# The second feed-forward product as seven block products in place of eight, in a two-layer hybrid decoder trunk

## The chip, the cores and the metric

The kernel is one program on one core of a Trainium2 chip. The time is that of the device for one launch, in microseconds; of the kernel before there are three runs, and their median counts.

## The reference

Each of two layers takes a stream x of 512 tokens x 1024 channels, float32. Three token mixers (gated spatial MLP, latent attention with eight heads, gated DeltaNet) read one normed input projection; their outputs are gated, merged, multiplied by W_out and added to x. Then comes the part that the change touches:

```
h2 = rms_norm(x, norm2_g[l])
x = x + jnp.square(jax.nn.relu(h2 @ w_ff1[l])) @ w_ff2[l]
```

w_ff1 is 1024 x 4096, w_ff2 4096 x 1024. The output is x after the second layer.

## The kernel before

**Precision.** Every large product is made in three passes over operands split into a high part (fp32r) and a low part (what the rounding left): high by high, high by low, low by high. `passes` (L454) issues the three. ScalarE or VectorE split the activations; GpSimd splits the weights, one unit of 128 x 1024 at a time: `high` (L424) copies the raw weights to wHi, `low` (L429) subtracts wHi from the raw ones into wLo. Raw units arrive by DMA in two slots, split ones stand in a ring of four. A unit is split when the unit four places earlier is done on TensorE.

**Layout.** The stream is channel-major: xT is 8 tiles of 128 channels x 512 tokens. The weights are stationary, the tokens move, 512 columns a matmul.

**The feed-forward block.** For each quarter of the 4096 hidden channels, TensorE makes eight hidden tiles (`ff1`, one unit and 24 matmuls each) and then eight units of the second product (`wide_sums`, L485, 24 matmuls each), which sums eight hidden tiles into eight banks of output channels. For a hidden tile, VectorE rectifies and scales it out of PSUM into relu (L2018), squares it back into PSUM (L2020) and subtracts the high part (L2023); ScalarE squares it into the high part (L1458). After a quarter VectorE adds eight banks to xT (L2034).

**Order.** Each engine has its own program, written out by hand, and executes it strictly in order; semaphores with absolute counts join them. No scheduler is used. The next norm's work hangs on the second product's end: `stream_low` on VectorE (adds the bank to xT, L1518, low part of h, L1504, accumulates squares, L1511) and `stream_high` on ScalarE (high part of h, copy to xT, square; L1115, L1116, L1109). The factor of the norm is applied after the product, so the next layer's first unit ("misc") begins before the statistic (`sum_stream`, L482) is known. At the very end `last_sums` interleaves the transposes back to token-major (`turn_out`, L542, L533), which ScalarE copies to ost and DMAs store.

## Time and profile before

| | us |
|---|---|
| median of three runs (1796.21 to 1796.32) | 1796.24 |
| profiled execution: span, first to last instruction | 1793.5 |
| profiled execution's own time: the page gives its span alone; median less span | 2.7 |
| TensorE busy | 1776.8 |
| GpSimd busy | 1030.1 |
| VectorE busy | 856.7 |
| ScalarE busy | 466.6 |
| granted TensorE clock, mean | 1.000 |

The busy shares add up every record of an engine, without counting an overlap twice. Matmuls overlap in the records: one is listed with its whole way through the array, though the next starts earlier. So a mean duration of a matmul isn't what it costs; the distance between starts is. The chain of waits is followed back from the last instruction. An idle time of an engine that isn't in the chain costs nothing.

### The profile page before, as it was taken

How to read it: one execution, taken by the hardware profiler on the slowest of the kernel's cores; microseconds unless marked ns; L12 is line 12 of the kernel's file. 1: busy time of each engine (PE TensorE's matmuls, PEld its weight loads, DVE VectorE, ACT ScalarE, POOL GpSimd, SP SyncE). 2: the span in 40 equal slices, each digit the busy share in tenths (PEclk: the TensorE clock that was granted, in tenths of full speed). 3: DMA queues.
4: the chain of work that ended last, by engine and by line, in shares of the span. 5: the costliest groups of instructions: out<-in, count | busy, mean ns of one | idle time of the engine just before them, and what ended most of it. 6: DMA issues, size and time to landing. Idle time of an engine off the chain costs nothing.

```text
span 1793.5 us, 26458 instructions
## 1 busy us (share of the span) xinstructions
PE 1776.8 (99%) x10078; PEld 1449.8 (81%) x10078; DVE 856.7 (48%) x1436; ACT 466.6 (26%) x922; POOL 1030.1 (57%) x580
## 2 busy tenths in 40 slices
PE   8999999999999999999999999999999999999999
PEld 7777888788888888888877788887888888888887
DVE  8786626644444231314276964466435351414141
ACT  6423317641113000000155142266311130001011
POOL 6543466255666666666664435652556666666663
PEclk9999999999999999999999999999999999999999
DMA  6222132132333333333342212320323333333332
GB/s 233 94 71 72 58 96 94 36 118 83 94 94 109 101 99 94 94 101 99 94 141 71 83 49 73 104 83 26 128 89 100 94 94 94 97 103 94 94 96 80
DMA packets 48439, 167.25 MB, mean 93 GB/s; under 512 B 5136, under 2 KB 10544, under 8 KB 47824
## 3 DMA queue, kind: packets, MB, share of 16 engines
q1 hardware_dynamic: 47024, 156.42, 28.1%
q10 hardware_dynamic: 1312, 9.33, 1.4%
q8 instruction: 80, 1.31, 0.3%
q14 instruction: 23, 0.19, 0.0%
HBM read 159.44 MB, written 6.29 MB: 92 GB/s over the span
## 4 chain that ended last, share of the span: by engine, by line
PE 94%; DVE 3%; ACT 2%; issue 1%; DMA 0%; SPq 0%; DVEq 0%; ACTq 0%
PE ps L461 28%; PE ps L463 27%; PE ps L462 27%; PE ps L967 2%; PE ps L976 1%; PE ps L989 1%; DVE acc L1511 1%; DVE hLo L1504 1%; PE ps L740 1%; PE ps L727 0%; PE ps L777 0%; DMA xin<-x 0%; PE ps L1039 0%; PE ps L763 0%; PE ps L752 0%
## 5 line engine op out<-in xcount | busy, mean ns | idle before, releaser
L429 POOL TENSOR_TENSOR wLo<-wraw,wHi 128x1024 fp32r<-128x1024 f32 x288 | 721.9, 2507 | 23.9
L424 POOL TENSOR_SCALAR wHi<-wraw 128x1024 fp32r<-128x1024 f32 x288 | 308.2, 1070 | 714.1 <-PE ps L463 698.4
L461 PE MATMUL ps<-hHi,wHi 128*128 128x512 f32 x1360 | 554.0, 407 | 1.3 <-DVE convd L1633 1.3
L463 PE MATMUL ps<-hHi,wLo 128*128 128x512 f32 x1360 | 530.4, 390 | 0.0
L462 PE MATMUL ps<-hLo,wHi 128*128 128x512 f32 x1360 | 529.8, 390 | 0.0
L461 PEld LDWEIGHTS ps<-hHi,wHi 128*128 128x128 f32 x1360 | 255.4, 188 | 61.7 <-issue 7.7
L462 PEld LDWEIGHTS ps<-hLo,wHi 128*128 128x128 f32 x1360 | 255.7, 188 | 55.4 <-issue 4.6
L463 PEld LDWEIGHTS ps<-hHi,wLo 128*128 128x128 f32 x1360 | 255.2, 188 | 54.5
L461 PE MATMUL ps<-fHi,wHi 128*128 128x512 f32 x640 | 249.3, 390 | 0.0
L463 PE MATMUL ps<-fHi,wLo 128*128 128x512 f32 x640 | 249.0, 389 | 0.0
L462 PE MATMUL ps<-fLo,wHi 128*128 128x512 f32 x640 | 249.0, 389 | 0.0
L1458 ACT ACTIVATE fHi<-relu 128x512 fp32r<-128x512 f32 x64 | 40.6, 635 | 555.3 <-DVE relu L2018 555.3
L2034 DVE TENSOR_TENSOR xT<-xT,ps 128x512 f32<-128x512 f32 (+1 forms) x57 | 38.6, 678 | 256.6 <-PE ps L463 256.6
L463 PEld LDWEIGHTS ps<-fHi,wLo 128*128 128x128 f32 x640 | 120.1, 188 | 25.1
L462 PEld LDWEIGHTS ps<-fLo,wHi 128*128 128x128 f32 x640 | 120.1, 188 | 24.8
L461 PEld LDWEIGHTS ps<-fHi,wHi 128*128 128x128 f32 x640 | 120.1, 188 | 24.8
L2018 DVE SCALAR_TENSOR_TENSOR relu<-ps,rstdT 128x512 f32<-128x512 f32 x64 | 44.3, 692 | 193.8 <-PE ps L463 185.9
L1166 ACT ACTIVATE sg<-ps 128x512 f32<-128x512 f32 x48 | 28.8, 600 | 255.7 <-DVE ps L1576 255.7
L1576 DVE TENSOR_TENSOR ps<-ps,rstdT 128x512 f32<-128x512 f32 x56 | 39.0, 699 | 111.2 <-PE ps L463 111.0
L463 PE MATMUL ps<-bHi,wLo 128*128 128x512 f32 x192 | 74.7, 389 | 0.0
L461 PE MATMUL ps<-bHi,wHi 128*128 128x512 f32 x192 | 74.7, 389 | 0.0
L462 PE MATMUL ps<-bLo,wHi 128*128 128x512 f32 x192 | 74.7, 389 | 0.0
(312 smaller groups left out, 1928.9 us busy)
## 6 DMA issues: line engine op xcount, KB each, us to landing
wraw<-stream SPq DMA_DIRECT2D x288, 512.0 KB, 3.5
out<-xT ACTq DMA_DIRECT2D x2, 2048.0 KB, 8.8
xT<-out ACTq DMA_DIRECT2D x2, 2048.0 KB, 8.6
xin<-x SPq DMA_DIRECT2D x4, 512.0 KB, 6.6
out<-ost SPq DMA_DIRECT2D x2, 512.0 KB, 3.0
out<-ost SPq DMA_DIRECT2D x3, 256.0 KB, 2.2
prm<-params ACTq DMA_DIRECT2D x1, 647.0 KB, 4.0
prm<-params SPq DMA_DIRECT2D x1, 576.0 KB, 8.9
```

Of the source, the lines that this page charges most:

```text
L424: nc.gpsimd.tensor_scalar(wHi[:, slot], wraw[:, slot % RAW], 1.0, 0.0, ALU.mult, ALU.add).then_inc(unit_high, 1)
L429: nc.gpsimd.tensor_tensor(wLo[:, slot], wraw[:, slot % RAW], wHi[:, slot].bitcast(F32), ALU.subtract).then_inc(unit_split, 1)
L461: mm(o, lh[lc], rh[rc], start=start, stop=False)
L462: mm(o, lh[lc], rl[rc], start=False, stop=False)
L463: return mm(o, ll[lc], rh[rc], start=False, stop=stop)
L740: last = mm(half_bank(half, 1)[hs(m), j % 2 * 64:j % 2 * 64 + 64], gated[hs(m), m // 2, 0, h], r[hs(m), j] if m else rhsv[hs(m), 0, h * 64 ...
L967: mm(bank[:, 0:w], qhT[0:QK, h, i * P:w], khT[0:QK, h, 0:w], start=True, stop=True).then_inc(score_done, 1)
L1166: f(gate[:, d % 2], bank_of(TILE_NO[tile]), ACT.Sigmoid).then_inc(bank_read[TILE_NO[tile] % 2], 1)
L1458: f(fHi[q % 2][:, n], relu[:, n % 2], ACT.Square).then_inc(f_hi, 1)
L1576: return tt_(o, bank_of(TILE_NO[tile]), rstdT[:], ALU.mult)
L2018: stt(relu[:, n % 2], bank_of(n), 0.0, rstdT[:], ALU.max, ALU.mult).then_inc(relu_done, 1)
L2034: tt_(xT[:, d][part], xT[:, d][part], sums_bank(d)[part], ALU.add).then_inc(x_added, 1)
```

## The change

The second product runs in 8 groups, each over four hidden tiles (512 hidden channels), on blocks of 256 tokens x 256 hidden channels by 256 hidden x 512 output channels. By hand that would be eight block products; Strassen's scheme in Winograd's form needs seven, of sums and differences of blocks. In the names: p1 to p7 are the seven products of a group, f0 to f3 the four hidden tiles of the next group that stand between them. A product is 2 token tiles x 2 hidden tiles x 3 passes = 12 matmuls of 512 columns. Now the activations are stationary and the weights move, and the result is token-major, in `y` (4 tiles of 128 tokens x 1024 channels).

- The hidden tiles are mixed on VectorE (`mix_halves`) and split into seven kinds of stationary blocks (fHi, fLo): kinds 0 and 1 from the first two tiles of a group, 2 to 6 from the last two (4 to 6 are the mixed ones).
- The weight blocks are loaded as four tiles (w11, w12, w21, w22). Their sums: B on GpSimd (`sum_upper`), T3 and T2 (`sum_lower`) and T4 (`sum_corners`) on VectorE.
- The high part of every weight unit from here on is copied by ScalarE (`high_part`), its low part made by GpSimd (`low_part`).
- The products of a chain share PSUM banks: X takes p1, p6, p7 and p4, one after another, and VectorE adds the bank to y after each (`add_corner`), 256 tokens at a time, in the last group 128.
- The stream is turned to token-major at the start of each feed-forward block (`turn_residual`: 32 transposes, four copies by ScalarE) and turned back between the layers (`turn_stream`). After the last layer y is stored as it is; `last_sums`, `turn_out` and the copies to ost are gone.
- Some semaphores are joined into others outside the block (vector_step); no instruction moves by that.

```diff
+PLACES = ("p1", "f0", "p5", "p6", "f1", "p2", "p7", "f2", "p3", "p4", "f3")
+LAST_PLACES = ("p2", "p1", "p6", "p7", "p4", "p5", "p3")
...
+            def low_part(layer, group, place, source):
+                at = split_no(group, place)
+                pool.wait_ge(high_copied, layer * per.high_copied + at - LEAD + 1)
+                nc.gpsimd.tensor_tensor(wLo[:, at % RING], source, wHi[:, at % RING].bitcast(F32), ALU.subtract).then_inc(unit_split, 1)
...
+                    sum_upper(layer, group)
+                    low_part(layer, group, "p1", w11[:])
+                    low_part(layer, group, "f0", ff1_raw(0))
+                    low_part(layer, group, "p5", b1112[:])
+                    low_part(layer, group, "p6", w11[:])
...
+                def turn_residual(t):
+                    bank = (2, 6, 4, 2)[t]
...
+                    for d in range(KD):
+                        last = nc.tensor.transpose(ps[:, bank + d // 4, d % 4 * P:(d % 4 + 1) * P], xT[:, d, t * P:(t + 1) * P], ident)
+                    last.then_inc(x_turned, 1)
...
+                def turn_stream(columns):
+                    for d in columns:
+                        if d == 0:
+                            pe.wait_ge(corner_added, added_count(layer, GROUPS - 1, "p4"))
+                        if d == 4:
+                            pe.wait_ge(corner_added, added_count(layer, GROUPS - 1, "p3"))
+                        if d == 6:
+                            pe.wait_ge(sq_ready, 8 * (2 * layer + 2) + 1)
                         if d == 7:
+                            pe.wait_ge(acc_step, 7 * (2 * layer + 2) + 1)
+                        for t in range(TT):
+                            last = nc.tensor.transpose(sums_bank(d)[:, t * P:(t + 1) * P], y[:, t, d * P:(d + 1) * P], ident)
...
+                def corner(group, place, kind, bank, opens, after=None):
+                    at = split_no(group, place)
+                    slot, b = at % RING, group % 2
+                    pe.wait_ge(unit_split, layer * per.unit_split + at + 1)
+                    if after and after[0] < GROUPS - 1:
+                        pe.wait_ge(corner_added, added_count(layer, *after))
+                    for i in range(2):
+                        if after and after[0] == GROUPS - 1:
+                            pe.wait_ge(corner_added, added_count(layer, *after, i))
+                        for k in range(2):
+                            tokens, cols = np.s_[:, kind, k, i * P:(i + 1) * P], np.s_[:, slot, k * 512:(k + 1) * 512]
+                            mm(ps[:, bank + i], fHi[b][tokens], wHi[cols], start=opens and k == 0, stop=False, skip_group_check=True)
+                            mm(ps[:, bank + i], fHi[b][tokens], wLo[cols], start=False, stop=False, skip_group_check=True)
+                            last = mm(ps[:, bank + i], fLo[b][tokens], wHi[cols], start=False, stop=k == 1, skip_group_check=True)
+                        if i == 0:
+                            last.then_inc(first_done, 1)
+                    last.then_inc(unit_done, 1)
...
+                    pe.wait_ge(vector_tile, vector_count(layer, 4 * g + 1, LOW_DONE))
+                    corner(g, "p1", 0, X, True, (g - 1, "p4") if g else None)
+                    ff1(4 * g + 4)
+                    pe.wait_ge(vector_tile, vector_count(layer, 4 * g + 3, LOW_MIXED))
+                    corner(g, "p5", 4, Y, True, (g - 1, "p3") if g else None)
...
+                    ff1(4 * g + 7)
+                g = GROUPS - 1
+                pe.wait_ge(vector_tile, vector_count(layer, 4 * g + 3, LOW_MIXED))
+                corner(g, "p2", 2, Z, False)
+                corner(g, "p1", 0, X, True, (g - 1, "p4"))
+                corner(g, "p6", 5, X, False, (g, "p1"))
+                corner(g, "p7", 1, X, False, (g, "p6"))
+                corner(g, "p4", 3, X, False, (g, "p7"))
+                corner(g, "p5", 4, Y, True, (g - 1, "p3"))
+                if layer < DEPTH - 1:
+                    turn_stream(range(0, 4))
+                corner(g, "p3", 6, Y, False, (g, "p5"))
+                if layer < DEPTH - 1:
+                    turn_stream(range(4, KD))
...
+                def square(n):
+                    act.wait_ge(vector_tile, vector_count(layer, n, RECTIFIED))
+                    ins = f(bank_of(n), relu[:, n % 2], ACT.Square)
+                    if n % 4 < 2:
+                        if n >= 4:
+                            act.wait_ge(vector_tile, vector_count(layer, n - 2, MIXED))
+                        ins = f(second[:, n % 2], relu[:, n % 2, 256:], ACT.Square)
+                    ins.then_inc(scalar_tile, 1)
+                def high_tile(n):
+                    k, b, halves = n % 2, n // 4 % 2, bank_of(n).rearrange("p (h t) -> p h t", h=2)
+                    act.wait_ge(vector_tile, vector_count(layer, n, MIXED))
+                    if n % 4 < 2:
+                        nc.scalar.copy(cross[:, k], bank_of(n)[:, 256:])
+                        nc.scalar.copy(fHi[b][:, 0:2, k], halves).then_inc(scalar_tile, 1)
+                    else:
+                        nc.scalar.copy(fHi[b][:, 2:4, k], halves).then_inc(scalar_tile, 1)
+                        nc.scalar.copy(fHi[b][:, 4:7, k], mixed[:]).then_inc(scalar_tile, 1)
...
+                    high_ff1(g, 3)
+                    square(n + 2)
+                    if g < GROUPS - 2:
+                        high_corner(g + 1, "p1")
+                        high_tile(n + 2)
+                        high_ff1(g + 1, 0)
+                        high_corner(g + 1, "p5")
+                    else:
+                        high_corner(g + 1, "p2")
+                        high_tile(n + 2)
+                        high_corner(g + 1, "p1")
...
+                def mix_halves(n):
+                    k, bank = n % 2, bank_of(n)
+                    dve.wait_ge(scalar_tile, scalar_count(layer, n, SQUARED))
+                    if n % 4 < 2:
+                        tt_(bank[:, 256:], bank[:, 0:256], second[:, k], ALU.subtract).then_inc(vector_tile, 1)
+                        return
+                    if n >= 3:
+                        dve.wait_ge(vector_tile, vector_count(layer, n - 1 if k else n - 3, LOW_MIXED))
+                    tt_(mixed[:, 0], bank[:, 256:], second[:, k], ALU.subtract).then_inc(vector_step, 1)
+                    stt(mixed[:, 1], bank[:, 256:], -1.0, cross[:, k], ALU.mult, ALU.subtract).then_inc(vector_step, 1)
+                    steps.next()
+                    dve.wait_ge(vector_step, steps.next())
+                    stt(mixed[:, 2], bank[:, 0:256], -1.0, mixed[:, 1], ALU.mult, ALU.subtract).then_inc(vector_tile, 1)
+                def low_tile(n):
+                    k, b, halves = n % 2, n // 4 % 2, bank_of(n).rearrange("p (h t) -> p h t", h=2)
+                    kinds = np.s_[:, 0:2, k] if n % 4 < 2 else np.s_[:, 2:4, k]
+                    dve.wait_ge(scalar_tile, scalar_count(layer, n, HIGH_DONE))
+                    tt_(fLo[b][kinds], halves, fHi[b][kinds].bitcast(F32), ALU.subtract).then_inc(vector_tile, 1)
+                    if n % 4 >= 2:
+                        dve.wait_ge(scalar_tile, scalar_count(layer, n, HIGH_MIXED))
+                        tt_(fLo[b][:, 4:7, k], mixed[:], fHi[b][:, 4:7, k].bitcast(F32), ALU.subtract).then_inc(vector_tile, 1)
+                def sum_lower(group):
+                    dve.wait_ge(w22_in, layer * per.corner_in + 16 * group + 16)
+                    dve.wait_ge(sum_b, layer * per.sum_b + group + 1)
+                    tt_(w12[:], w12[:], w22[:], ALU.add).then_inc(sums_done, 1)
+                    dve.wait_ge(sums_done, sums_count(layer, group, T3))
+                    dve.wait_ge(unit_split, layer * per.unit_split + split_no(group, "p1") + 1)
+                    tt_(w11[:], w11[:], w12[:], ALU.add).then_inc(sums_done, 1)
+                def sum_corners(group):
+                    dve.wait_ge(unit_split, layer * per.unit_split + split_no(group, "p2") + 1)
+                    dve.wait_ge(sums_done, sums_count(layer, group, T2))
+                    tt_(w21[:], w21[:], w11[:], ALU.add).then_inc(sums_done, 1)
...
+                        part = y[:, 2 * row:2 * row + 2, cols]
+                        tt_(part, part, ps[:, bank:bank + 2], op).then_inc(corner_added, 1)
...
+                    rectify(n + 2)
+                    add_corner(g, "p3", Y, 0, 1, ALU.subtract, (g, "p6"))
+                    mix_halves(n + 2)
+                    add_corner(g, "p4", X, 1, 0, ALU.add, (g - 1, "p4") if g else None)
+                    low_tile(n + 2)
+                    sum_lower(g + 1)
+                    rectify(n + 3)
+                    if g == GROUPS - 2:
+                        sum_corners(g + 1)
+                    mix_halves(n + 3)
+                    low_tile(n + 3)
...
+                add_corner(g, "p5", Y, 1, 1, ALU.subtract, (g, "p7"))
+                add_corner(g, "p3", Y, 0, 1, ALU.subtract, (g, "p6"))
+                if layer < DEPTH - 1:
+                    stream_low(2 * layer + 2, 0, 0)
...
-                        tt_(bank_of(n), relu[:, n % 2], relu[:, n % 2], ALU.mult).then_inc(fsq_step, 1)
...
-                                tt_(xT[:, d][part], xT[:, d][part], sums_bank(d)[part], ALU.add).then_inc(x_added, 1)
```

On VectorE, in the feed-forward block before, this stands around the end of a quarter:

```order
L2018 SCALAR_TENSOR_TENSOR relu<-ps,rstdT 128x512 [waits f_lo,unit_done]
L2020 TENSOR_TENSOR ps<-relu 128x512 [waits relu_done]
L2023 TENSOR_TENSOR fLo<-ps,fHi 128x512 [waits f_hi,fsq_step]
L2034 TENSOR_TENSOR xT<-xT,ps 128x512 [waits sums_full] x3
L2034 TENSOR_TENSOR xT<-xT,ps 128x512 [waits unit_done]
L2034 TENSOR_TENSOR xT<-xT,ps 128x512 [waits sums_full] x3
L2034 TENSOR_TENSOR xT<-xT,ps 128x512 [waits unit_done]
```

And now, where a turn ends (third hidden tile's parts, T3 and T2 of the next group, then the fourth hidden tile). `w<-w` are the sums of weight blocks, `y<-y,ps` adds a product:

```order
L2325 TENSOR_TENSOR y<-y,ps 128x2x512 [waits unit_done,corner_added]
L2297 TENSOR_TENSOR fLo<-ps,fHi 128x2x256 [waits scalar_tile]
L2300 TENSOR_TENSOR fLo<-mixed,fHi 128x3x256 [waits scalar_tile]
L2306 TENSOR_TENSOR w<-w 128x1024 [waits sum_b,w22_in]
L2309 TENSOR_TENSOR w<-w 128x1024 [waits unit_split,sums_done]
L2275 SCALAR_TENSOR_TENSOR relu<-ps,rstdT 128x512 [waits scalar_tile,unit_done]
L2286 TENSOR_TENSOR mixed<-ps,second 128x256 [waits vector_tile,scalar_tile]
L2287 SCALAR_TENSOR_TENSOR mixed<-ps,cross 128x256
L2290 SCALAR_TENSOR_TENSOR mixed<-ps,mixed 128x256 [waits vector_step]
L2297 TENSOR_TENSOR fLo<-ps,fHi 128x2x256 [waits scalar_tile]
L2300 TENSOR_TENSOR fLo<-mixed,fHi 128x3x256 [waits scalar_tile]
```

The two sums, both with two inputs in SBUF, stand ahead of the rectifying of the fourth hidden tile.

On TensorE the entry of the last group: the last matmuls of hidden tile 31, and p2 directly behind them, which waits for `vector_tile`, the count of that same tile's mixed low part (in the other groups p1 and f0 stand between):

```order
L613 MATMUL ps<-hHi,wHi 128x512
L614 MATMUL ps<-hLo,wHi 128x512
L615 MATMUL ps<-hHi,wLo 128x512
L1229 MATMUL ps<-wHi,fHi 128x512 [waits unit_split,vector_tile]
L1230 MATMUL ps<-wLo,fHi 128x512
L1231 MATMUL ps<-wHi,fLo 128x512
L1229 MATMUL ps<-wHi,fHi 128x512
```

Before, the first unit of the second product stood there, and waited for the quarter's first two hidden tiles, done six units earlier.

And on TensorE between the layers, behind the last product p3: the transposes of channels 4 to 7 wait for VectorE's sum of p3, for ScalarE's first square and for VectorE's first accumulation, and stand ahead of the next layer's first unit.

```order
L681 MATMUL ps<-cst,y 128x128 [waits corner_added]
L681 MATMUL ps<-cst,y 128x128 x7
L681 MATMUL ps<-cst,y 128x128 [waits sq_ready]
L681 MATMUL ps<-cst,y 128x128 x3
L681 MATMUL ps<-cst,y 128x128 [waits acc_step]
L681 MATMUL ps<-cst,y 128x128 x3
L613 MATMUL ps<-hHi,wHi 128x512 [waits h_lo,unit_split]
L614 MATMUL ps<-hLo,wHi 128x512
L615 MATMUL ps<-hHi,wLo 128x512
```

Before, nothing stood between the last matmul of the second product and the first of the next layer.

## Rows read from the trace of the kernel before

**Rows 1.** The page: busy us (share) xinstructions by engine; the chain's shares by engine.
```profile
PE 1776.8 (99%) x10078; PEld 1449.8 (81%) x10078; DVE 856.7 (48%) x1436; ACT 466.6 (26%) x922; POOL 1030.1 (57%) x580
...
PE 94%; DVE 3%; ACT 2%; issue 1%; DMA 0%; SPq 0%; DVEq 0%; ACTq 0%
```

**Rows 2.** The page, costliest groups: busy us, mean ns of one.
```profile
L461 PE MATMUL ps<-fHi,wHi 128*128 128x512 f32 x640 | 249.3, 390 | 0.0
```

**Rows 3.** Timeline of TensorE: start us, us, engine, line, operation, tiles [idle before].
```profile
5.24 3.37 PE L475 MATMUL ps<-cst,xin 128*128 128x128 f32 x16 [5.24 <-DMA xin<-x]
...
600.07 0.39 PE L461 MATMUL ps<-fHi,wHi 128*128 128x512 f32 x1
...
601.66 0.39 PE L462 MATMUL ps<-fLo,wHi 128*128 128x512 f32 x1
```

**Rows 4.** Two stretches: length, busy us (xinstructions) by engine, granted clock, DMA.
```profile
0.00:11.00 11.00, 4.99 (x24) 4.26 (x25) 4.79 (x14) 5.86 (x10) 2.89 (x7) 1.00 0.85 298
549.00:899.00 350.00, 349.79 (x1541) 288.98 (x1541) 111.30 (x146) 37.72 (x61) 230.35 (x129) 1.00 0.32 99
```

**Rows 5.** Timeline of TensorE: key/value up-projection, and transposes in the last product.
```profile
273.20 0.39 PE L461 MATMUL ps<-wHi,latHi 128*128 128x512 f32 x1
...
273.88 0.39 PE L461 MATMUL ps<-wHi,latHi 128*128 128x512 f32 x1
...
1769.81 1.91 PE L542 MATMUL ps<-cst,xT 128*128 128x128 f32 x16
1771.47 0.48 PE L461 MATMUL ps<-fHi,wHi 128*128 128x512 f32 x1
1771.79 0.39 PE L462 MATMUL ps<-fLo,wHi 128*128 128x512 f32 x1
```

**Rows 6.** Timeline of GpSimd, then VectorE, where the branches are merged.
```profile
501.68 2.39 POOL L429 TENSOR_TENSOR wLo<-wraw,wHi 128x1024 fp32r<-128x1024 f32 x1
...
507.06 2.71 POOL L429 TENSOR_TENSOR wLo<-wraw,wHi 128x1024 fp32r<-128x1024 f32 x1
...
512.63 2.70 POOL L429 TENSOR_TENSOR wLo<-wraw,wHi 128x1024 fp32r<-128x1024 f32 x1
...
507.43 2.88 DVE L1605 TENSOR_TENSOR fLo<-merged,fHi 128x512 fp32r<-128x512 f32 x1
...
510.95 0.69 DVE L1600 TENSOR_TENSOR merged<-merged,gy 128x512 f32<-128x512 f32 x1
```

**Rows 7.** Groups by form, VectorE and ScalarE: busy us, mean ns of one.
```profile
L2018 DVE SCALAR_TENSOR_TENSOR relu<-ps,rstdT 128x512 f32<-128x512 f32 x64 | 44.3, 692 | 193.8 <-PE ps L463 185.9 <-ACT rstdT L1126 7.9
...
L2034 DVE TENSOR_TENSOR xT<-xT,ps 128x256 f32<-128x256 f32 x2 | 0.8, 418 | 5.7 <-PE ps L463 5.7
...
L1171 ACT CAST fHi<-merged 128x512 fp32r<-128x512 f32 x14 | 8.7, 618 | 47.6 <-DVE merged L1600 47.6
...
L1334 ACT CAST bHi<-oval 128x1536 fp32r<-128x1536 f32 x2 | 3.0, 1482 | 10.4 <-DVE oval L1790 10.4
```

**Rows 8.** Timeline of VectorE, then ScalarE, one hidden tile.
```profile
643.11 0.69 DVE L2018 SCALAR_TENSOR_TENSOR relu<-ps,rstdT 128x512 f32<-128x512 f32 x1 [4.75 <-PE ps L463]
...
643.84 0.63 ACT L1458 ACTIVATE fHi<-relu 128x512 fp32r<-128x512 f32 x1 [48.33 <-DVE relu L2018]
```

**Rows 9.** Timeline of ScalarE, then TensorE, between the layers.
```profile
897.30 0.69 ACT L1115 ACTIVATE hHi<-ps,prm 128x512 fp32r<-128x512 f32 x1 [0.20 <-DVE ps L1518]
897.89 0.57 ACT L1116 COPY xT<-ps 128x512 f32<-128x512 f32 x1
898.36 0.60 ACT L1109 ACTIVATE ps<-ps 128x512 f32<-128x512 f32 x1
...
904.40 1.12 PE L482 MATMUL ps<-acc,cst 128*128 128x512 f32 x2 [0.21 <-DVE acc L1511]
```

**Rows 10.** Timeline of TensorE, then ScalarE, at the program's end.
```profile
1789.11 0.40 PE L463 MATMUL ps<-fHi,wLo 128*128 128x512 f32 x1
...
1790.50 0.70 ACT L1470 COPY ost<-ps 128x256 f32<-128x256 f32 x2 [1.76 <-PE ps L533]
```

More of the change, by code:

```diff
@@ L137 @@
 class PerLayer:
[L140 removed]
+    unit_split = SPLITS; unit_done = SPLITS
     x_stored = 16; prm_loaded = 16; x_loaded = 16
@@ L415, in _, with load_front, load_ff1 @@
-            sp.wait_ge(ost_copied, 8)
-            sp.dma_start(out[0:2 * P, 7 * P:].rearrange("(t p) d -> p t d", p=P), ost[:, 0:2, 7 * P:]).then_inc(out_stored, 16)
+            def load_front(layer):
+                with sp.Fori(1, LEAD // RAW) as turn:
+                    n = turn * RAW
+                    for slot in range(RAW):
+                        sp.wait_ge(unit_split, layer * per.unit_split + n + slot - RAW + 1)
+                        load_unit(layer * U + n + slot, slot)
+            def load_ff1(layer, n, split):
+                sp.wait_ge(unit_split, layer * per.unit_split + split + 1)
+                if n < 32:
+                    load_unit(layer * U + UNIT_NO[("ff1", n)], n % 2)
+                elif layer < DEPTH - 1:
+                    load_unit((layer + 1) * U + n - 32, n % 2)
@@ new lines, in _, with store @@
+            final = DEPTH - 1
+            def store(t, tokens, half):
+                cols = np.s_[half * 512:(half + 1) * 512]
+                sp.dma_start(out[t * P:(t + tokens) * P, cols].rearrange("(t p) d -> p t d", p=P), y[:, t:t + tokens, cols]).then_inc(out_stored, 16)
+            last = GROUPS - 1
+            sp.wait_ge(corner_added, added_count(final, last, "p1"))
+            store(0, 2, 0)
+            sp.wait_ge(corner_added, added_count(final, last, "p4"))
+            store(2, 2, 0)
@@ L418, in _ @@
+            sp.wait_ge(corner_added, added_count(final, last, "p5"))
+            store(2, 2, 1)
+            for i in range(2):
+                sp.wait_ge(corner_added, added_count(final, last, "p3", i))
+                store(i, 1, 1)
         @block.gpsimd
@@ new lines, in _, with ff1 @@
+                        wide_sums(half, kk)
+                def ff1(n):
+                    at = ff1_no(n)
+                    slot = at % RING
+                    if n < 2:
+                        pe.wait_ge(bank_read[n], (layer + 1) * per.bank_read)
+                    else:
+                        pe.wait_ge(vector_tile, vector_count(layer, n - 2, LOW_DONE if n % 4 >= 2 else LOW_MIXED))
+                    pe.wait_ge(unit_split, layer * per.unit_split + at + 1)
+                    for k in range(KD):
+                        if n == 0:
+                            pe.wait_ge(h_lo, layer * per.h_lo + 8 + k + 1)
+                        last = passes(bank_of(n), (wHi, wLo), np.s_[:, slot, k * P:(k + 1) * P], (hHi, hLo), np.s_[:, k], k == 0, k == KD - 1)
+                    last.then_inc(unit_done, 1)
@@ new lines, in copy_residual @@
+                def copy_residual(t):
+                    bank = (2, 6, 4, 2)[t]
+                    act.wait_ge(x_turned, 8 + layer * per.x_turned + t + 1)
+                    nc.scalar.copy(y[:, t], ps[:, bank:bank + 2].rearrange("p b n -> p (b n)")).then_inc(residual_copied, 1)
+                copy_residual(0)
+                copy_residual(1)
+                square(0)
+                high_tile(0)
+                high_corner(0, "p1")
+                copy_residual(2)
+                copy_residual(3)
```

425 lines of the change are left out of this document (259 added, 166 removed).

## The prediction

> **What bounds the kernel now.** I began with the page's busy shares and its chain of waits [rows 1]: TensorE is busy for 1776.8 of 1793.5 us and makes 94% of the chain, VectorE 3%. So time is saved by giving TensorE fewer columns, and lost wherever it is made to wait. Next I read the matmul groups by form and TensorE's timeline in the feed-forward block [rows 2, 3]. A matmul of 512 columns is recorded with 389 ns, but the starts stand 0.227 us apart (seven steps from 600.07 to 601.66 take 1.59 us). The step is the price, not the record. A load unit of 24 matmuls is 5.44 us. In the window that holds the first layer's feed-forward block TensorE is busy 349.79 of 350 us [rows 4]; VectorE works 111 of it, ScalarE 38, GpSimd 230. No wait is to be had back there; the change can only remove columns, and must not open waits. Then I read the shortest pieces of every engine that the new code uses, and last how VectorE and GpSimd get in each other's way [rows 6].
>
> The page gives the span, 1793.5 us. The runs have a median of 1796.24, so 2.7 us lie around the span; I take that as fixed and add differences of the span to the median.
>
> **Columns removed.** The second product costs 8 products x 4 x 3 = 96 matmuls per group of four hidden tiles, 768 per layer. The new form costs 7 x 12 = 84, 672 per layer. So 192 matmuls go in two layers: 192 x 0.2267 = 43.5 us. The stationary operand is now the activations and the moving one the weights. The trace has that arrangement already, in the key/value up-projection: 0.39 us recorded, the same as the others, and three steps from 273.20 to 273.88 take 0.68, so 0.227 each [rows 5]. I take the same step, +43.5 saved; half a per cent of 0.227 over the 1344 matmuls left would be 1.5 us.
>
> **Transposes.** Sixteen stand 1.66 us from first to next start, and the matmul behind them is followed after 0.32 instead of 0.23 [rows 5]: 1.75 us a block of 16, and by the same step 0.51 a block of 4. Gone: one block of 16 and three of 4 inside the last product, 3.3 us. New: per layer two blocks that turn the residual to token-major, and two between the layers: 6 x 1.75 = 10.5. Net +7.2 us.
>
> **The other engines.** Here are the pieces that I use. VectorE with one PSUM input: 0.69 us for 512 columns, 0.42 for 256 [rows 7], so by their slope 1.22 for 1024. ScalarE: 0.62 for 512, 1.48 for 1536 [rows 7], so 1.05 for 1024, 0.83 for 768. Hand-over between engines is about 0.04, read where the square starts 0.04 behind the rectified tile [rows 8]. GpSimd: 2.39 per low part when undisturbed [rows 6]. A turn of the new loop is 4 units of 24 matmuls and 7 of 12, 40.8 us. In it GpSimd has 12 pieces of 2.39 = 28.7 us, VectorE some 24, ScalarE some 20. By throughput all of it is hidden. By order it isn't.
>
> **The price of a shared port.** At 507.06 a low part begins on GpSimd, at 507.43 VectorE's subtraction of two SBUF tiles. It takes 2.88 us where one of the same size at 510.95, with GpSimd idle, takes 0.69, and ends at 510.31, some 0.54 behind GpSimd's end at 509.77 [rows 6]. At 512.63 the order is the other way and GpSimd takes 2.70 instead of 2.39. So of a VectorE instruction with two SBUF inputs and a low part, the later one stands still; the one that comes first wins, and the other starts about 0.14 before its end. With PSUM as one input there is no such delay (0.69 throughout). The change brings five instructions of the first kind a turn: T3, T2 and T4, sums of weight blocks of 1024 columns (1.21 each), and two low parts of mixed tiles (768 columns, 0.95). The Trainium skill's page "SBUF — State Buffer", section "Who interferes with whom", calls this a lock held for the full instruction, with issue order deciding. If the port were shared by bandwidth instead, each would lose a fraction and the stall worked out next would go, with the sum at some 1785; the trace here agrees with the lock.
>
> **A turn walked through.** Clock 0 is the end of the third hidden tile (f2). TensorE then needs 2.7 for p3, 2.7 for p4, 5.4 for f3, so f3 ends at 10.9; 2.7 for p1 of the next group and 5.4 for f0 bring it to p5 at 19.0. p5 waits for the mixed low part of the tile f3.
> - VectorE: rectifies (0.2 to 0.9), adds p3 (2.9 to 4.1), mixes in three steps (to 5.3), adds p4 (5.6 to 6.9), low part (to 7.5), mixed low part (7.4 to 8.3). ScalarE's copies follow the mix: 5.3 to 6.6, then the high part of f0 to 7.6.
> - GpSimd takes f0's low part at 8.2 (it queued first, at 7.7) and holds the port to 10.6. T3 arrives at 8.3 and runs 10.5 to 11.7. GpSimd's low part of p5 queued meanwhile, 11.5 to 13.9. T2 runs 13.8 to 15.0.
> - Only then VectorE rectifies the tile that was ready at 10.9: to 15.6, square 16.3, mix 17.5, ScalarE's two copies 18.9. The mixed low part meets p6's low part (17.3 to 19.7) and ends at 20.5. p5 starts 1.5 late.
> With 0.1 for refilling TensorE, 1.6 us x 6 turns x 2 layers = 19.2. Without the port the same walk has no stall; with every dependence 0.1 longer it is 2.5. Bounds: 0 and 30.
>
> **Entry of the last group.** There p2 stands directly behind the last hidden tile and waits for its mixed low part, with no p1 and f0 between. From that tile's end: T3 until 0.8, T2 1.9, rectify 2.5, T4 3.7, mix 4.8, copies 6.1, then the wait for p7's low part (6.0 to 8.4), end 9.2. TensorE idles 9.2 + 0.2 = 9.4, twice: 18.8. Without the port 5.7 each, 11.4; upper bound 11 each. The kernel before started its sums there with tiles finished long before, and has no idle time.
>
> **Between the layers.** Before, the sums of the stream come one by one and the next layer's h is made beside the last matmuls: TensorE waits 0.21 us for the accumulated squares, 0.36 with what lies around it, before the statistic at 904.40 [rows 9]. Now VectorE's adding of p3 stands before all eight h pieces. From p3's end at 0: add done 0.9, transposes, first low h 1.6. From there ScalarE sets the pace with three pieces a tile, 0.59 + 0.47 + 0.60 = 1.66 start to start [rows 9]: the eighth low h at 12.5, the statistic at 13.9. TensorE has 1.75 + 5.44 = 7.2 us of work there. Idle 6.7 for 0.36: +6.3 us. Bounds 3 and 9.
>
> **Start and end.** In the first group of a layer p6 waits 0.14 for T2: 0.3 in all. Filling y, and the residual's copies on ScalarE (four of about 1.1), end before ff1(2) and ff1(3) ask, by 0.9 and 1.0 us. At the end the chain was matmul, sum, transposes, copy, store: last matmul start 1789.11, copy's end 1791.20, span's end 1793.5 [rows 10]. Now it is matmul, sum of 0.69, store of the same 256 KB: about 1.0 us shorter.
>
> **Sum.** -43.5 + 7.2 + 19.2 + 18.8 + 6.3 + 0.3 - 1.0 = +7.3. Median 1796.2 + 7.3 = 1803.5; I say 1804.
>
> **Rivals.**
> - *The stalls in the turns don't come* (faster). If T3 or T2 slips in before a low part, 2.4 us of delay go, more than the 1.5 of the stall. Then +7.3 - 19.2 = -11.9: 1784.3; with the last group's entry short as well (7.4 less), -19.3: 1777. For it: throughput is ample, and one step of the walk (7.7 against 8.3) is close. Against: T2 always finds p5 queued. 24%.
> - *Half of them* (no change): 0.8 a turn saves 9.6, and 8 at each entry 2.8 more: 1791 to 1794. 12%.
> - *TensorE falls to its lower clock in the gaps* (slower than I say). The granted clock is 1.00 in every window of before [rows 4], the first 11 us with the one long wait of 5.24 us among them [rows 3]. But that stands before all matmuls, not between them. If the 24 matmuls behind each 9.4 us gap ran at 1.2 GHz they'd cost 5.4 more, 10.9 in all: 1815. 7%. The Trainium skill's page "TensorE: Matmul & The Clock Gate", section "What's actually happening", has an idle array fall back to 1.2 GHz; by it this case would be the likeliest, and no row here shows it.
> - *It doesn't do what it says*: the matmuls with activations stationary step slower. 2% more (0.005 us x 1344 = 6) gives 1810. 4%.
> - My forecast: 53%, its own range 1798 to 1812.
>
> **How the numbers follow.** A measurement of this kernel tells 0.2%, 3.6 us, from no change: same is 1792.6 to 1799.8. Faster: 24% and 2 of the 12. Same: 9 of the 12 and 5 of my own case. Slower: the rest, 60%. The range reaches from the middle of the fast case to the clock case: 1781 to 1813.
>
> **What would show it.** Right: T3 and T2 with 2 to 3.5 us each and not 1.2; TensorE's idle time of 1 to 2 us before p5 in groups 1 to 6, released by the mixed low part; 9 us before p2 of group 7; six or seven in pieces between the layers. Wrong: if the step of the block products isn't 0.227, if GpSimd's low parts stand at 2.39 through the block, if the gaps are elsewhere (a load not there, p6 waiting for the sum of p1), or if granted clock under 1.00 stands behind a gap.

## The result: 0.7% slower

The changed kernel takes 1809.68 us (median of 4 runs, 1809.41 to 1810.08), the kernel before 1796.28 us in the same session. The ratio is 1.0073, 95% interval 1.006 to 1.0086. The forecast was 1804, range 1781 to 1813, with 60% on slower. The span of the profiled execution is 1808.3 us against 1793.5, so 14.8 us more; the difference of the medians is 13.4. The two don't contradict each other: wherever a run has both, its time is 1.8 us above its span (1810.08 and 1808.3 here; 1795.94 and 1794.1 for a run of the kernel before). So the 1793.5 belong to an execution of about 1795.3 us (an estimate), 0.9 under its median, and the 1808.3 to one 0.4 over its own. The 2.7 us that the prediction laid around the span are 1.8 and this 0.9.

The page of the changed kernel, busy us by engine and the chain's shares (answers to [rows 1]):

```profile
PE 1752.6 (97%) x9950; PEld 1423.6 (79%) x9950; DVE 1060.3 (59%) x1627; ACT 707.3 (39%) x1249; POOL 1060.5 (59%) x524
...
PE 79%; DVE 12%; ACT 4%; issue 4%; POOL 0%; DMA 0%; DVEq 0%; ACTq 0%
```

TensorE's busy time falls by 24.2 us and the span still grows. VectorE now makes 12% of the chain, before 3%. The table of waits of TensorE says who held it up (us in total, times, longest):

```profile
PE ps L1229 <- DVE fLo L2300: 35.1, 14, 9.1
```

Fourteen waits for the mixed low part (L2300): twelve of 1.34 to 1.43 us inside the groups and two of 9.1 us at the last groups. The stretches of the first layer's block (length, busy by engine, granted clock; the first row answers to [rows 4]):

```profile
549.00:899.00 350.00, 332.16 (x1457) 271.70 (x1456) 205.21 (x232) 151.65 (x213) 237.99 (x96) 0.99 0.27 92
872.00:881.40 9.40, 0.41 (x2) 0.00 (x0) 8.64 (x9) 3.83 (x5) 5.11 (x3) 0.78 0.00 0
881.40:886.00 4.60, 4.52 (x11) 3.55 (x12) 1.27 (x4) 0.00 (x0) 0.00 (x0) 0.50 0.00 0
...
892.00:906.00 14.00, 13.64 (x68) 10.90 (x66) 5.91 (x10) 3.28 (x5) 12.36 (x8) 1.00 0.21 69
```

In the long gap VectorE is the busy one, 8.64 of 9.40 us. And behind it the granted clock is 0.50, that is 1.2 GHz, where [rows 4] have 1.00 throughout. TensorE's timeline there, and behind an ordinary wait inside a group:

```profile
669.37 0.50 PE L1229 MATMUL ps<-wHi,fHi 128*128 128x512 f32 x1 [1.43 <-DVE fLo L2300]
669.70 0.39 PE L1230 MATMUL ps<-wLo,fHi 128*128 128x512 f32 x1
...
881.48 0.79 PE L1229 MATMUL ps<-wHi,fHi 128*128 128x512 f32 x1 [9.07 <-DVE fLo L2300]
882.07 0.63 PE L1230 MATMUL ps<-wLo,fHi 128*128 128x512 f32 x1
...
887.19 0.52 PE L1230 MATMUL ps<-wLo,fHi 128*128 128x512 f32 x1
887.55 0.39 PE L1231 MATMUL ps<-wHi,fLo 128*128 128x512 f32 x1
...
889.16 0.39 PE L1229 MATMUL ps<-wHi,fHi 128*128 128x512 f32 x1
...
891.88 0.39 PE L1229 MATMUL ps<-wHi,fHi 128*128 128x512 f32 x1
```

From 882.07 to 887.19 the starts stand 0.427 us apart; later (889.16 to 891.88, twelve steps) 0.2267, the step of [rows 3, 5]. Fourteen matmuls take 6.07 us from 881.48, where at the pace behind the short wait (0.33, then about 0.23 each) they would take 3.3: the fall costs 2.8 us. In the second layer thirteen take 5.61 from 1783.10, where 3.1 would do: 2.5 us. Behind the waits of 1.4 us there is none.

One turn, followed back by the chain (start us, us, what): it is the walk of the prediction, on the chip; between the rectifying and ScalarE's copy (L1673) stand the square and three mixing steps.

```profile
657.13 3.35 DVE w L2306
...
660.64 3.09 issue
663.73 0.69 DVE relu L2275
...
666.81 0.85 ACT fHi L1673
...
667.68 1.64 DVE fLo L2300
...
669.37 0.50 PE ps L1229
```

The "issue" of 3.09 us isn't idle time: VectorE's and GpSimd's timelines of the same stretch show it inside the sum T2 (L2309).

```profile
657.05 3.42 DVE L2306 TENSOR_TENSOR w<-w 128x1024 f32<-128x1024 f32 x1
660.50 3.31 DVE L2309 TENSOR_TENSOR w<-w 128x1024 f32<-128x1024 f32 x1
663.73 0.68 DVE L2275 SCALAR_TENSOR_TENSOR relu<-ps,rstdT 128x512 f32<-128x512 f32 x1
...
656.45 2.94 POOL L569 TENSOR_TENSOR wLo<-wraw,wHi 128x1024 fp32r<-128x1024 f32 x1 [2.73 <-ACT wHi L1638]
659.35 3.38 POOL L569 TENSOR_TENSOR wLo<-b,wHi 128x1024 fp32r<-128x1024 f32 x1
```

T3 waits until GpSimd's low part of f0 is over (659.39) and ends 1.1 us later; GpSimd's low part of p5 then waits for T3, and T2 for it. T3 and T2 are recorded with 3.4 and 3.3 us for 1.22 us of work each (the time that e1 below shows for them). It is the alternation of [rows 6], and the rectifying that was due behind it starts at 663.73.

The long gap ends the way the prediction walked it: the mixed low part stands still until GpSimd has finished two low parts in a row (875.51 to 880.61), and p2 starts behind it.

```profile
878.60 2.83 DVE L2300 TENSOR_TENSOR fLo<-mixed,fHi 128x768 fp32r<-128x768 f32 x1
...
875.51 5.10 POOL L569 TENSOR_TENSOR wLo<-w,wHi 128x1024 fp32r<-128x1024 f32 x2 [3.50 <-ACT wHi L1638]
```

Between the layers TensorE waits in six pieces, five of them here (answers to [rows 9]):

```profile
906.49 1.09 PE L681 MATMUL ps<-cst,y 128*128 128x128 f32 x8 [0.85 <-DVE y L2335]
...
910.22 0.66 PE L681 MATMUL ps<-cst,y 128*128 128x128 f32 x4 [1.78 <-DVE acc L1768]
915.87 0.51 PE L613 MATMUL ps<-hHi,wHi 128*128 128x512 f32 x1 [0.60 <-DVE hLo L1761]
917.43 0.50 PE L613 MATMUL ps<-hHi,wHi 128*128 128x512 f32 x1 [0.58 <-DVE hLo L1761]
918.82 1.13 PE L634 MATMUL ps<-acc,cst 128*128 128x512 f32 x2 [0.42 <-DVE acc L1768]
```

The statistic starts at 918.82 where it stood at 904.40 [rows 9]. So of the 14.8 us by which the span grew, 14.4 lie before it, in the first layer. The second layer has the same waits in the groups and at the last one, but no turning between layers behind it, and about breaks even.

### The profile page after: what moved, and what is told of

Read it like the earlier page. It is cut to its first block, busy times and chain, and to the rows that moved or that the text cites. A ratio compares the mean times of both kernels' runs of the same rounds, so it can differ in the third digit from the quotient of the medians.

```text
span 1808.3 us, 26198 instructions
## 1 busy us (share of the span) xinstructions
PE 1752.6 (97%) x9950; PEld 1423.6 (79%) x9950; DVE 1060.3 (59%) x1627; ACT 707.3 (39%) x1249; POOL 1060.5 (59%) x524
## 4 chain that ended last, share of the span: by engine, by line
PE 79%; DVE 12%; ACT 4%; issue 4%; POOL 0%; DMA 0%; DVEq 0%; ACTq 0%
PE ps L613 18%; PE ps L615 18%; PE ps L614 18%; PE ps L1229 5%; PE ps L1231 5%; PE ps L1230 5%; DVE w L2306 3%; DVE fLo L2300 2%; PE ps L1106 2%; PE ps L1115 1%; PE ps L1128 1%; DVE y L2325 1%; ACT fHi L1673 1%; DVE convd L1890 1%; DVE acc L1768 1%
## 5 line engine op out<-in xcount | busy, mean ns | idle before, releaser
L538 POOL TENSOR_SCALAR wHi<-wraw 128x1024 fp32r<-128x1024 f32 x168 | 181.5, 1080 | 501.1 <-PE ps L615 484.9
L543 POOL TENSOR_TENSOR wLo<-wraw,wHi 128x1024 fp32r<-128x1024 f32 x168 | 415.2, 2471 | 13.9
L569 POOL TENSOR_TENSOR wLo<-w,wHi 128x1024 fp32r<-128x1024 f32 x96 | 231.5, 2421 | 172.2 <-ACT wHi L1638 172.2
L1229 PE MATMUL ps<-wHi,fHi 128*128 128x512 f32 x448 | 178.7, 399 | 35.3 <-DVE fLo L2300 35.1
L1230 PE MATMUL ps<-wLo,fHi 128*128 128x512 f32 x448 | 176.5, 394 | 0.0
L1231 PE MATMUL ps<-wHi,fLo 128*128 128x512 f32 x448 | 176.4, 394 | 0.0
L2325 DVE TENSOR_TENSOR y<-y,ps 128x1024 f32<-128x1024 f32 x84 | 102.4, 1219 | 119.2 <-PE ps L1231 119.2
L569 POOL TENSOR_TENSOR wLo<-wraw,wHi 128x1024 fp32r<-128x1024 f32 x56 | 146.6, 2618 | 41.2 <-ACT wHi L1638 41.2
L1229 PEld LDWEIGHTS ps<-wHi,fHi 128*128 128x128 f32 x448 | 85.4, 191 | 59.8 <-DVE fLo L2300 41.0
L1638 ACT CAST wHi<-w 128x1024 fp32r<-128x1024 f32 x96 | 100.2, 1044 | 37.9 <-PE ps L1231 20.3
L1230 PEld LDWEIGHTS ps<-wLo,fHi 128*128 128x128 f32 x448 | 85.5, 191 | 17.5
```

Source lines behind the costliest of these rows:

```text
L538: nc.gpsimd.tensor_scalar(wHi[:, slot], wraw[:, slot % RAW], 1.0, 0.0, ALU.mult, ALU.add).then_inc(unit_high, 1)
L543: nc.gpsimd.tensor_tensor(wLo[:, slot], wraw[:, slot % RAW], wHi[:, slot].bitcast(F32), ALU.subtract).then_inc(unit_split, 1)
L569: nc.gpsimd.tensor_tensor(wLo[:, at % RING], source, wHi[:, at % RING].bitcast(F32), ALU.subtract).then_inc(unit_split, 1)
L1229: mm(ps[:, bank + i], fHi[b][tokens], wHi[cols], start=opens and k == 0, stop=False, skip_group_check=True)
L1230: mm(ps[:, bank + i], fHi[b][tokens], wLo[cols], start=False, stop=False, skip_group_check=True)
L1231: last = mm(ps[:, bank + i], fLo[b][tokens], wHi[cols], start=False, stop=k == 1, skip_group_check=True)
```

## Experiments

All start from the changed kernel. Its own ratio to the kernel before, 1.0073, is what they are read against; every ratio below is to the kernel before, run on the same chip in the same session. The theory: TensorE is held up because VectorE's sums of weight blocks and GpSimd's low parts take turns, with the rectifying queued behind them. The rivals: the dependence through mixing and copying is too long without them, or the block products are dearer than they look.

**e1: the sums late.** VectorE's T3 and T2 (and T4 of the last group) go behind the last tile's low parts, so they no longer stand before the rectifying.

```diff
                     low_tile(n + 2)
+                    rectify(n + 3)
+                    mix_halves(n + 3)
+                    low_tile(n + 3)
                     sum_lower(g + 1)
-                    rectify(n + 3)
                     if g == GROUPS - 2:
                         sum_corners(g + 1)
-                    mix_halves(n + 3)
-                    low_tile(n + 3)
```

(ScalarE's high parts of p6, and of p7 in the last group, go behind high_tile(n + 3) to match.)

> T3, T2 (and T4 of the last group) stand behind the fourth hidden tile's low parts instead of ahead of its rectifying; ScalarE copies p6's weights behind that tile's high parts. Theory (order and shared port): the waits of 1.42 us before p5 go, with their refill 12 x 1.7 = 20.4 us; the entry of the last group waits 5.5 instead of 9.07, 7.1 more in two; p6 may wait 0.1 to 0.2 a turn, 1.7 back. 1809.7 - 20.4 - 7.1 + 1.7 = 1784. Rival (the engines are too full, the order doesn't matter): the waits move to p6 and the time stays within 5 us of 1809.7.

Measured: 1785.56 us, ratio 0.9941 (0.9925 to 0.9958). TensorE's waits, then T3 by form:

```profile
PE ps L1229 <- DVE fLo L2300: 10.0, 2, 5.0
```

```profile
L2306 DVE TENSOR_TENSOR w<-w 128x1024 f32<-128x1024 f32 x16 | 19.5, 1220 | 0.0
```

The twelve waits are gone, the two long ones have 5.0 us, and the same instruction takes 1.22 us where it took 3.14 on the mean. The kernel is 24 us faster than as changed, and faster than before: the columns' gain was there all along. The granted clock still falls behind the 5.0 us. The late sums have a price too: p6 now starts 0.27 us late in seven groups of each layer (its weights come late) and is 0.14 more behind after its first matmuls, 0.4 us fourteen times or 5.7, where the changed kernel pays that in the first groups alone and I had expected 1.7.

**e2: the sums with one input.** This parts the collision from the place: the order stays.

```diff
-                    tt_(w12[:], w12[:], w22[:], ALU.add).then_inc(sums_done, 1)
+                    nc.vector.reduce_sum(w12[:], w12[:].unsqueeze(2), AX.X).then_inc(sums_done, 1)
...
-                    tt_(w11[:], w11[:], w12[:], ALU.add).then_inc(sums_done, 1)
+                    nc.vector.reduce_sum(w11[:], w11[:].unsqueeze(2), AX.X).then_inc(sums_done, 1)
```

> T3 and T2 are instructions of the same place, size and own duration (about 1.2 us for 1024 columns), but read one SBUF tile instead of two: a reduction over an axis of length one, which leaves the second summand out of the weight sums. Theory (the port): they take 1.2 us each instead of 3.1 and 2.8, the 1.42 us waits go (20.4 us), the entry waits about 8.3 instead of 9.07 (1.5 us): 1788. Rival (they only stand in the way by their own length): a turn loses at most what remains of 2 x 1.2 us, the waits stay near 1.4 and the time near 1809.

Measured: 1786.87 us, ratio 0.9946 (0.9929 to 0.9963). Waits, T3 and the mixed low part, then VectorE and GpSimd in a turn:

```profile
PE ps L1229 <- DVE fLo L2300: 16.1, 2, 8.1
```

```profile
L2306 DVE TENSOR_REDUCE w<-w 128x1024 f32<-128x1024 f32 x16 | 19.4, 1214 | 0.0
...
L2300 DVE TENSOR_TENSOR fLo<-mixed,fHi 128x768 fp32r<-128x768 f32 x32 | 42.5, 1329 | 0.7
```

```profile
655.70 1.22 DVE L2306 TENSOR_REDUCE w<-w 128x1024 f32<-128x1024 f32 x1
656.95 1.22 DVE L2309 TENSOR_REDUCE w<-w 128x1024 f32<-128x1024 f32 x1
...
655.10 2.95 POOL L569 TENSOR_TENSOR wLo<-wraw,wHi 128x1024 fp32r<-128x1024 f32 x1 [2.73 <-ACT wHi L1638]
658.01 2.40 POOL L569 TENSOR_TENSOR wLo<-b,wHi 128x1024 fp32r<-128x1024 f32 x1
```

With one input VectorE works right through GpSimd's instruction, and GpSimd's next is undisturbed. The mixed low part still collides (1329 ns, as changed 1320), and no wait comes of it. So it is T3 and T2 that make the twelve waits. The time fell by 22.8 us; the entries are 1.0 us shorter each, so some 20.8 are the price of the twelve waits, forecast at 19.2.

**e8: the mirror, GpSimd with one input.**

```diff
-                nc.gpsimd.tensor_tensor(wLo[:, at % RING], source, wHi[:, at % RING].bitcast(F32), ALU.subtract).then_inc(unit_split, 1)
+                nc.gpsimd.tensor_scalar(wLo[:, at % RING], source, 1.0, 0.0, ALU.mult, ALU.add).then_inc(unit_split, 1)
```

> The mirror of e2_sums_one_input. The changed kernel with VectorE's sums as they are (two inputs), and GpSimd's low parts of the block units (wLo of w, wraw and b) written by tensor_scalar from one input in place of tensor_tensor from two: it leaves out that subtraction, so the low parts hold the blocks themselves. GpSimd's instruction falls from 2.4 to some 1.1 us. Theory, that T2 and T3 wait for GpSimd's two-input instructions and GpSimd's for them: T3 and T2 take 1.22 us, the 12 waits of 1.4 us go, the last group's wait is 8 us or less as in e2, 1785 to 1788 us. Rival, that VectorE's sums are slow by any work of GpSimd on the shared memory: T2 and T3 stay over 2 us, the waits stay at least in part, 1795 to 1810.

Measured: 1781.33 us, ratio 0.9912 (0.9895 to 0.9929). No wait inside the groups, 5.85 us at the last ones. But T3 and T2 do not take 1.22 us. VectorE, then GpSimd:

```profile
655.04 2.07 DVE L2306 TENSOR_TENSOR w<-w 128x1024 f32<-128x1024 f32 x1
657.15 1.95 DVE L2309 TENSOR_TENSOR w<-w 128x1024 f32<-128x1024 f32 x1
...
654.45 1.60 POOL L569 TENSOR_SCALAR wLo<-wraw 128x1024 fp32r<-128x1024 f32 x1 [4.08 <-ACT wHi L1638]
656.01 2.02 POOL L569 TENSOR_SCALAR wLo<-b 128x1024 fp32r<-128x1024 f32 x1
```

In the mean of all sixteen they take 1.96 and 1.77 us. My theory was wrong in this point, and the rival right in it, though not in its waits and its 1795 us or more: one-input work on GpSimd (1.05 us undisturbed) and two-input work on VectorE still take turns. GpSimd ends at 656.05, T3 at 657.11, GpSimd at 658.03, T2 at 659.10: 1.06, 0.92 and 1.07 us each after the last. The time fell all the same, below the 1785 expected, because what each waits for is now 1.05 us and not 2.4: T3 and T2 together take 2.7 us less than in the changed kernel, more than the 1.4 of a wait, and each entry is 3.2 us shorter. What parts the two engines is VectorE's second input, not GpSimd's. The Trainium skill's page "SBUF — State Buffer", section "Who interferes with whom", says as much: a VectorE instruction with two SBUF inputs contends with a GpSimd instruction that reads SBUF, one with at most one such input, outside what the page calls the 2-port modes, doesn't. e2 and e8 agree with both halves.

**e3: the last group begins with p1.** p1 needs only tiles that are long ready; it goes in front of p2, whose wait for the mixed low part it should shorten.

```diff
-LAST_PLACES = ("p2", "p1", "p6", "p7", "p4", "p5", "p3")
+LAST_PLACES = ("p1", "p2", "p6", "p7", "p4", "p5", "p3")
...
+                pe.wait_ge(vector_tile, vector_count(layer, 4 * g + 1, LOW_DONE))
+                corner(g, "p1", 0, X, True, (g - 1, "p4"))
                 pe.wait_ge(vector_tile, vector_count(layer, 4 * g + 3, LOW_MIXED))
                 corner(g, "p2", 2, Z, False)
-                corner(g, "p1", 0, X, True, (g - 1, "p4"))
```

(The other engines take p1 and p2 of the last group in the new order too.)

> In the last group p1 stands ahead of p2; it needs only the first two hidden tiles. The turns stay. Theory: p1's 2.7 us cover part of the entry, the wait is 4.4 to 6.3 us instead of 9.07 and stands before p2, so 5.5 to 9.3 us less in two layers: 1800 to 1804. If the clock also stays at 2.4 GHz behind the shorter wait, 5.6 more: 1795. Rival (p1's own weights come too late in the last group): the wait moves to p1 and nothing is won.

Measured: 1802.86 us, ratio 1.0037 (1.0023 to 1.0051). The long waits are 6.35 us each instead of 9.1, the twelve of 1.4 stay. p1's own 12 matmuls (2.72 us) come off each, 5.4 us in two: nearly all of the 5.6 by which the span is shorter (the medians differ by 6.8). The clock fell again behind the wait.

**e4: useless matmuls in the long gap.** 32 matmuls into a free bank, ahead of p2 of the last group; their result is used nowhere. It asks what the clock costs.

```diff
+                def fill(count):
+                    pe.wait_ge(vector_tile, vector_count(layer, 4 * GROUPS - 2, LOW_MIXED))
+                    for i in range(count):
+                        mm(bank_of(0), hHi[:, 0, 0:P], hHi[:, 1], start=True, stop=True)
...
+                fill(32)
```

> 32 matmuls of no use (into a PSUM bank that nobody reads again) fill most of the 9.07 us before p2 of the last group. All waits stay. Theory (clock): the 13 matmuls behind the gap step 0.227 instead of 0.427 us, 2.8 us a layer: 1804. Rival (the slow matmuls come from the products themselves or from refilling): 1809.7, with the same 0.427.

Measured: 1808.45 us, single runs from 1805.55 to 1809.61, ratio 1.0065 (1.0048 to 1.0082): not told apart from the changed kernel by its interval. The profiled run says why. The wait is 1.90 us now in both layers; in the first the matmuls behind it go at full speed, in the second they fall after all, 1.6 us later:

```profile
882.00 0.50 PE L1229 MATMUL ps<-wHi,fHi 128*128 128x512 f32 x1 [1.90 <-DVE fLo L2307]
...
1781.09 0.50 PE L1229 MATMUL ps<-wHi,fHi 128*128 128x512 f32 x1 [1.90 <-DVE fLo L2307]
...
1782.67 0.63 PE L1229 MATMUL ps<-wHi,fHi 128*128 128x512 f32 x1
```

The fastest run has the mean granted clock 0.999, the two slowest 0.997, the changed kernel 0.994. So the filling keeps the clock in some gaps and not in others. That the clock can be kept is shown once, in one gap; what it would give in every gap was not reached. The rival is out by the same gap: p2's matmuls there step by 0.23 us (882.33, 882.57, 882.80). The profiled span is 2.1 us shorter than the changed kernel's; 0.9 of what was gained goes again behind the last matmul (4.6 us to the end for 3.7), for a reason that I don't know.

The granted clock also falls once between the layers, for 3.4 us: in e4 it is 0.50 from 908.7 to 912.0, and e1, e2, e3, e6 and e8 have the same, while the changed kernel, e5 and e7 don't. It costs nothing there. From p3's last matmul to the statistic it takes 13.57 us in each of the six as in the changed kernel, because ScalarE and VectorE set the pace.

**e5: the boundary in another order.** The first two units of the next layer read rows that no longer change. VectorE splits them ahead of its last add of p3. (`stream_low` takes a fourth argument: 0 for the first part of its loop, 1 for the rest. ScalarE gets one wait more ahead of its own pieces, for the split of p3's weights.)

```diff
+                if layer < DEPTH - 1:
+                    stream_low(2 * layer + 2, 0, 0, 0)
...
-                    stream_low(2 * layer + 2, 0, 0)
+                    stream_low(2 * layer + 2, 0, 0, 1)
```

> The changed kernel with one thing done at the boundary of the layers: VectorE splits the first two of the next layer's units (which read rows that no longer change) ahead of its last add of p3, in place of behind it. Theory, that the 14.2 us which the changed kernel lost between the last group and sum_stream is a chain of VectorE's work behind the one batch of sums of eight units, with p3's add and split in its middle: some 3.3 us shorter, so about 1806 us; the waits of 1.78 and 0.60 us behind the acc and hLo rows shrink. Rival, that TensorE waits there for the last unit's statistics whatever the order: 1809 to 1810, no change.

Measured: 1806.01 us, ratio 1.0049 (1.0034 to 1.0065), the span 3.9 us shorter than the changed kernel's. The intervals of the two ratios just touch (1.0060 to 1.0065), so the timeline has to show the gain. TensorE's:

```profile
906.14 1.96 PE L681 MATMUL ps<-cst,y 128*128 128x128 f32 x16 [0.85 <-DVE y L2338]
912.40 0.50 PE L613 MATMUL ps<-hHi,wHi 128*128 128x512 f32 x1 [0.19 <-DVE hLo L1762]
913.97 0.50 PE L613 MATMUL ps<-hHi,wHi 128*128 128x512 f32 x1 [0.59 <-DVE hLo L1762]
915.35 1.13 PE L634 MATMUL ps<-acc,cst 128*128 128x512 f32 x2 [0.42 <-DVE acc L1769]
```

The transposes go in one piece, the wait of 1.78 us for acc is gone, and from them to the statistic it takes 9.21 us instead of 12.33: 3.1 us, as the theory said. Of the two waits of 0.6 behind hLo, which I expected to shrink, one has 0.19 left and the other 0.59.

**e6 and e7: together.** e6 has e1's and e3's edits, e7 e5's as well.

> The late sums of e1_sums_late together with the last group's order p1, p2 of e3_p1_first. The 12 waits inside the groups stay away (e1). At the last group the one wait of 5.0 us becomes two shorter ones, about 2.8 us ahead of p2 and 2.0 ahead of p6. Theory on the clock, that a gap long enough (5 us and over in e1 and in the changed kernel) makes TensorE fall to 1.2 GHz behind it, and that gaps under 3 us do not (1.42 us did not): no stretch at 0.50 behind them, and 1785.6 - 2 x (0.2 + 2.8) = about 1779.5. Rival, that it is the idle share of the stretch and not the single gap that counts: the fall stays, about 1785.

> e6_late_p1 and e5_boundary in one kernel. If the three repairs are independent, their gains add: e6's time less some 3.3 us, 1776 if the clock stays at 2.4 GHz, 1782 if it falls as in e1. Rival: with the turns' waits gone the boundary is another (VectorE arrives there earlier), and the split ahead of the add gives nothing: e6's time.

Measured: e6 1784.11 us, ratio 0.9934 (0.9919 to 0.9949); e7 1781.06 us, ratio 0.9918 (0.9905 to 0.9932). In e6's entry to the last group there are now two waits, 2.29 us for the mixed low part and 1.38 for a low part of GpSimd, and the clock falls behind the first:

```profile
869.88 0.79 PE L1229 MATMUL ps<-wHi,fHi 128*128 128x512 f32 x1 [2.29 <-DVE fLo L2301]
...
873.39 0.39 PE L1231 MATMUL ps<-wHi,fLo 128*128 128x512 f32 x1
...
875.84 0.50 PE L1229 MATMUL ps<-wHi,fHi 128*128 128x512 f32 x1 [1.38 <-POOL wLo L569]
```

So my threshold, no fall under 3 us, is refuted. The fall is short: from 869.88 to 873.39 eight steps take 3.51 us where 1.95 would do. In e7's first layer the matmuls behind the same 2.29 us start at full speed. Its timeline there, and between the layers:

```profile
869.85 0.50 PE L1229 MATMUL ps<-wHi,fHi 128*128 128x512 f32 x1 [2.29 <-DVE fLo L2304]
875.80 0.60 PE L1229 MATMUL ps<-wHi,fHi 128*128 128x512 f32 x1 [2.92 <-POOL wLo L569]
...
894.14 1.97 PE L681 MATMUL ps<-cst,y 128*128 128x128 f32 x16 [0.85 <-DVE y L2339]
903.36 1.12 PE L634 MATMUL ps<-acc,cst 128*128 128x512 f32 x2 [0.42 <-DVE acc L1770]
```

There the fall comes behind the second wait, of 2.92 us. The length of the gap alone doesn't decide it.

The lines of 875.84 and 875.80 also say in good part why e6 isn't at the 1779.5 of its theory. p6 starts at 875.84 with a fall before it and at 875.80 without: it waits for GpSimd's low part, and what the matmuls before it gain by a full clock only makes its wait longer (2.92 for 1.38). So the fall in e6's entry costs nothing, and keeping the clock there would have won nothing. That e6's 1784 lies near its rival's 1785 is no proof of that rival.

e7's span is 1.5 us under e6's and its median 3.1 under; the intervals of the two overlap. The trace shows both halves: from the transposes to the statistic e7 takes 9.22 us where e6 takes 12.33 (892.63 to 904.96), the same 3.1 us as in e5, and the fall behind its longer wait gives 1.6 back. e7 is the fastest that computes all of the reference: faster than the kernel before by 0.8%, where the change by itself was slower by 0.7%.

## Why the prediction was right

*Side and mechanism.* The chain of the turn came as walked: low part of f0, T3, low part of p5, T2, rectifying, mixing, copies, mixed low part, p5. e1 and e2 take it away in two ways, and the twelve waits go with it.

*Columns.* 0.2267 a step was right: twelve steps of 2.72 us above. With the waits gone in e1 the kernel is below the one before. "It doesn't do what it says" is out.

*Waits inside the groups.* The stall was put at 1.5 us. The table's 1.34 to 1.43 count from the end of the 0.39 us record; by starts, p5 comes 1.73 to 1.82 us after the matmul before it where 0.23 was due, so 1.5 to 1.6 late. The first matmuls behind it add 0.14 (0.33 for the first step, 0.23 to 0.235 for some more), put at 0.1. A turn was put at 40.8 + 1.6 = 42.4 and takes 42.52 (626.85 to 669.37 between the starts of two p5). All twelve cost 20.5 instead of 19.2.

*Entry of the last group.* 9.2 forecast; by starts p2 comes 9.23 late, with 0.14 behind it: 18.8 with both layers, as forecast. The step that the prediction named last, the wait for GpSimd's low part, is the one that ends it.

*Between the layers.* From p3's last matmul start at 905.25, plus its step, to the statistic at 918.82: 13.3 us, forecast 13.9. So +5.7 for +6.3. ScalarE sets the pace, as the prediction had it, with 1.55 us a tile and not 1.66 (its high parts start at 907.62, 909.17 and 910.72).

*End.* From the last matmul's start to the span's end 4.4 us before [rows 10] and 3.7 now (1804.62 to 1808.3): -0.7 for -1.0.

*The clock.* This is the step that was mis-sized. The rival priced it at 10.9 us with 7%; it came, at half that price, 2.8 + 2.5 = 5.3 us, in all four runs of the changed kernel (mean granted clock 0.993 to 0.994). I had taken 24 matmuls behind each gap, and 13 or 12 ran slow. Its chance was the worse error: [rows 3, 4] hold no gap between matmuls of more than a fraction of a microsecond, so they could say nothing for or against, and 7% was read out of silence. The Trainium skill's page "TensorE: Matmul & The Clock Gate", section "What's actually happening", made it the likeliest; behind the two gaps of 9.07 us the measurement agrees with the page.

*The sum* by measured sizes: -43.5 + 7.2 + 20.5 + 18.8 + 0.8 + 5.7 + 5.3 - 0.7 = +14.1, where 7.2 (transposes) is the forecast's own and 0.8 is p6 of the first groups (0.27 late and 0.14 behind that, twice, against 0.3). These sizes are the profiled execution's, so they stand against the 14.8 of the spans; 0.7 us stay unassigned. The forecast of +7.3 was 6.8 short of that sum: 5.3 by the clock, 1.3 by the waits in the groups, 0.5 by p6 and 0.3 by the end, less 0.6 between the layers.

*Rivals.* "The stalls don't come", 1784.3: no. Its price was about right, by e2 (20.8 us for the 19.2 put on the twelve waits). e1's 1785.56 lies close to 1784.3 by chance: it also holds 8.1 us won at the entries and 4.9 lost at p6. I gave the rival 24% for a lucky order; TensorE waited in all twelve.

## What to carry to other kernels

Fewer columns on the bounding engine pay only if the engines that feed it keep their order: walk one turn instruction by instruction, and look above all at what an instruction of another purpose (here two sums with time to spare) stands in front of. A VectorE instruction with two SBUF operands beside a busy GpSimd costs not only its own time but also what is left of GpSimd's; put it where nothing urgent is queued behind, or give it an operand elsewhere. Where a change opens the first gap of several microseconds between matmuls, count the lower clock behind it as likely: a trace without gaps is no evidence against it. And ask what the next wait is for: where another engine sets it, a slower clock ahead of it costs nothing.
